# Two more row tile pairs of the down projection in a seven-product scheme, with the activation sums moved from GpSimd to VectorE and some transposes placed later

## The reference, cut to what matters

```python
h2 = rms_norm(x, ln_ffn_w[i])
u = causal_depthwise_conv(h2 @ w_up[i], conv_w[i], conv_b[i])
u_gate, u_val = jnp.split(u, 2, axis=-1)
x = x + (jax.nn.silu(u_gate) * u_val) @ w_down[i]
h3 = rms_norm(x, ln_ple_w[i])
x = x + jax.nn.sigmoid(h3 @ w_ple_gate[i]) * (p[i] @ w_ple[i])
```

## Time and profile before

| what | value |
|---|---|
| median of 3 runs | 1438.42 us (1438.13 to 1439.0) |
| profiled execution, its own time | 1438.39 us |
| its span | 1436.6 us, so 1.8 us lie around the span |
| mean granted TensorE clock | 0.999 of full speed |
| busy: TensorE matmul, VectorE, ScalarE, GpSimd | 1425.5, 985.1, 760.0, 216.9 us |

### The profile page before, as it was taken

How to read it: one execution, slowest core, us unless ns; L and a number is a source line. 1 busy time by engine, 2 the same in 40 slices (tenths; PEclk the granted TensorE clock), 3 DMA queues, 4 the chain that set the end, 5 groups by cost and what they waited for, 6 DMA issues and landing times.

```text
span 1436.6 us, 19705 instructions
## 1 busy us (share of the span) xinstructions
PE 1425.5 (99%) x7112; PEld 1212.1 (84%) x7112; DVE 985.1 (69%) x1180; ACT 760.0 (53%) x920; POOL 216.9 (15%) x153
## 2 busy tenths in 40 slices
PE   9999999999999999999999999999999999999997
PEld 7888888888888888888888888888888888888886
DVE  7576777845455455566777777777777887787755
ACT  7555655544444444555555555555555546554544
POOL 0044144100000000000101101111011531140000
PEclk9999999999999999999999999999999999999999
DMA  9765555456666655465666566565665656565653
GB/s 325 225 205 161 165 176 159 143 194 190 191 190 191 191 190 188 158 208 181 190 188 191 180 198 186 179 204 175 191 193 177 212 192 200 177 213 188 227 200 121
DMA packets 190875, 273.47 MB, mean 190 GB/s; under 512 B 11744, under 2 KB 103136, under 8 KB 190688
## 3 DMA queue, kind: packets, MB, share of 16 engines
q1 hardware_dynamic: 190384, 272.30, 59.6%
q10 hardware_dynamic: 432, 0.37, 0.1%
HBM read 270.53 MB, written 2.10 MB: 190 GB/s over the span
## 4 chain that ended last, share of the span: by engine, by line
PE 98%; DVE 1%; issue 1%; ACT 0%; ACTq 0%; POOLq 0%; POOL 0%; DVEq 0%
PE main L622 15%; PE main L624 15%; PE main L623 15%; PE aux L747 11%; PE main L747 11%; PE aux L756 6%; PE main L756 6%; PE main L672 3%; PE main L670 3%; PE main L671 3%; PE aux L670 3%; PE aux L672 3%; PE aux L671 3%; PE aux L788 1%; PE aux L818 1%
## 5 line engine op out<-in xcount | busy, mean ns | idle before, releaser
L1301 DVE TENSOR_TENSOR w_lo<-raw,w_hi 128x1024 fp32r<-128x1024 f32 (+1 forms) x490 | 612.4, 1260 | 394.5 <-ACT w_hi L1009 394.3
L1009 ACT ACTIVATE w_hi<-raw 128x1024 fp32r<-128x1024 f32 (+1 forms) x490 | 514.1, 1052 | 541.2 <-PE main L624 284.8
L622 PE MATMUL main<-w_hi,xT 128*128 128x512 f32 x702 | 276.8, 394 | 0.0
L624 PE MATMUL main<-w_hi,xT 128*128 128x512 f32 x702 | 273.6, 390 | 0.0
L623 PE MATMUL main<-w_lo,xT 128*128 128x512 f32 x702 | 273.6, 390 | 0.0
L747 PE MATMUL aux<-xT,w_hi 128*128 128x512 f32 x704 | 169.9, 391 | 0.0
L747 PE MATMUL main<-xT,w_hi 128*128 128x512 f32 x672 | 163.0, 391 | 0.0
L624 PEld LDWEIGHTS main<-w_hi,xT 128*128 128x128 f32 x702 | 131.9, 188 | 27.4
L622 PEld LDWEIGHTS main<-w_hi,xT 128*128 128x128 f32 x702 | 132.0, 188 | 27.0 <-issue 0.4
L623 PEld LDWEIGHTS main<-w_lo,xT 128*128 128x128 f32 x702 | 132.0, 188 | 26.1
L747 PEld LDWEIGHTS aux<-xT,w_hi 128*128 128x128 f32 x704 | 129.4, 188 | 25.2 <-issue 0.3
(11 more groups left out here) (270 smaller groups left out, 1770.7 us busy)
## 6 DMA issues: line engine op xcount, KB each, us to landing
raw<-in_w_up SPq DMA_DIRECT2D x336, 256.0 KB
raw<-in_w_in SPq DMA_DIRECT2D x136, 512.0 KB
raw<-in_w_down SPq DMA_DIRECT2D x84, 512.0 KB
raw<-in_w_out SPq DMA_DIRECT2D x32, 512.0 KB
raw<-in_w_ple_gate SPq DMA_DIRECT2D x32, 512.0 KB
raw<-in_w_branch_a SPq DMA_DIRECT2D x16, 512.0 KB
raw<-in_w_branch_b SPq DMA_DIRECT2D x16, 512.0 KB
raw<-in_w_in SPq DMA_DIRECT2D x15, 256.0 KB, 5.7
```

The source lines that it names most:

```text
L622: pe.matmul(acc, th, wh, start=first, stop=False)
L624: return pe.matmul(acc, tl, wh, start=False, stop=end)
L1009: ac.activation(w_hi[:, u % RING, :, 0:w], raw[:, u % RING, :, 0:w], ACT.Copy).then_inc(hi_full, 1)
L1301: dve.tensor_tensor(w_lo[:, u % RING, :, 0:w], raw[:, u % RING, :, 0:w], w_hi[:, u % RING, :, 0:w].bitcast(F32), ALU.subtract).then_inc(lo ...
```

## The change

- `SEVEN_AT` has six pairs a pass, at i = 5, 7, 10, 12, 15, 17, in place of five, at 5, 8, 11, 14, 17. So a seven-product pair is followed by one or by two plain pairs in turn, where there were two each time.
- Of the activation sums GpSimd keeps the join of high and low part (`join_act`). The four 128 by 128 additions go to VectorE (`act_sums`), in slot u - 4 (`SUMS_AT`; for the very first pair slot u - 2, as slot 8 of the stage is the earliest). ScalarE rounds them and VectorE takes the low part in slot u - 3. The results have two buffers, and the semaphore of the weight sums is split in two (`w_diffs`, `w_summed`).
- The transposes of the new x come one unit later, with the scaling behind them one slot later, and so do those of `obT` for head group 1, by two units.

```diff
-OBT = [PV[g] + 4 for g in range(2)]
+OBT = [PV[g] + 4 + 2 * g for g in range(2)]
...
-SEVEN_AT = ((5, 8, 11, 14, 17), (5, 8, 11, 14, 17))
+SEVEN_AT = ((5, 7, 10, 12, 15, 17), (5, 7, 10, 12, 15, 17))
 SEVENS = [down_unit(p, i) for p in range(2) for i in SEVEN_AT[p]]
 SEVEN = {u: q for q, u in enumerate(SEVENS)}
+SUMS_AT = {max(u - 4, DOWN + UK): q for q, u in enumerate(SEVENS)}
...
-X2_AT = {down_slot(n) + 1: n for n in range(NQ)}
+X2_AT = {down_slot(n) + 2: n for n in range(NQ)}
...
-        a_sums_hi = sb("a_sums_hi", [P, 4, P], F32R, ffn)
-        a_sums_lo = sb("a_sums_lo", [P, 4, P], F32R, ffn)
+        a_sums_hi = sb("a_sums_hi", [P, 2, 4, P], F32R, ffn)
+        a_sums_lo = sb("a_sums_lo", [P, 2, 4, P], F32R, ffn)
...
                 if part == 0:
                     ac.wait_ge(a_summed, q + 1)
-                    if q:
-                        ac.wait_ge(w_sums_done, 2 * q)
+                    if q > 1:
+                        ac.wait_ge(w_sums_done, 2 * (q - 1))
...
+                if s - 1 in SUMS_AT:
+                    sums_hi(SUMS_AT[s - 1], 0)
                 if s + 1 in SEVEN:
-                    sums_hi(SEVEN[s + 1], 0)
                     sums_hi(SEVEN[s + 1], 1)
...
-                        if s == at + 2:
+                        if s == at + 1 + norm:
                             hi_blocks(name, xT_hi, 4 * n, VCOL[vec] + 4 * n, xT_hi_ready)
...
+            def act_sums(q):
+
+                dve.wait_ge(a_joined, q + 1)
+                a = a_sums[:].rearrange("p k (b t) -> p k b t", t=P)
+                a11, a12, a21, a22 = a[:, 0, 0], a[:, 1, 0], a[:, 0, 1], a[:, 1, 1]
+                dve.tensor_tensor(a22, a21, a22, ALU.add).then_inc(a_sum_part, 1)
+                dve.wait_ge(a_sum_part, 3 * q + 1)
+                dve.tensor_tensor(a21, a11, a21, ALU.subtract).then_inc(a_sum_part, 1)
+                dve.wait_ge(a_sum_part, 3 * q + 2)
+                dve.tensor_tensor(a11, a22, a11, ALU.subtract).then_inc(a_sum_part, 1)
+                dve.wait_ge(a_sum_part, 3 * q + 3)
+                dve.tensor_tensor(a12, a12, a11, ALU.subtract).then_inc(a_summed, 1)
...
                     split_lo(s + LEAD)
+                if s in SUMS_AT:
+                    act_sums(SUMS_AT[s])
                 if s + 2 in SEVEN:
-                    weight_sums(s + 2)
-                if s + 1 in SEVEN:
-                    sums_lo(SEVEN[s + 1], 0)
+                    weight_diffs(s + 2)
+                if s - 1 in SUMS_AT:
+                    sums_lo(SUMS_AT[s - 1], 0)
                 for k in range(2):
                     if s - k in SEVEN:
                         sums_lo(SEVEN[s - k], k + 1)
...
-                        if s == at + 2:
+                        if s == at + 1 + norm:
                             lo_blocks(name, xT_lo, xT_hi, 4 * n, VCOL[vec] + 4 * n, xT_hi_ready, xT_ready, 4 * (NQ * norm + n))
...
-            def act_sums(u, q):
+            def join_act(u, q):
...
                 pool.tensor_tensor(a_sums[:], aT_hi[:, k:k + 2, :].bitcast(F32), aT_lo[:, k:k + 2, :].bitcast(F32),
-                                   ALU.add).then_inc(a_sum_part, 1)
-                pool.wait_ge(a_sum_part, done + 1)
-                pool.tensor_tensor(a22, a21, a22, ALU.add).then_inc(a_sum_part, 1)
+                                   ALU.add).then_inc(a_joined, 1)
```

More of the change, by code:

```diff
@@ L355, in build @@
             sem, ("pT_hi_ready", "pT_ready", "sig_ready", "emb_ready", "y_pre"))
[L357 to L360, removed]
+        w_diffs, w_summed, w_sums_hi_ready, w_sums_ready, w_sums_done = map(
+            sem, ("w_diffs", "w_summed", "w_sums_hi_ready", "w_sums_ready", "w_sums_done"))
+        a_joined, a_sum_part, a_summed, a_sums_hi_ready, a_sums_ready = map(
+            sem, ("a_joined", "a_sum_part", "a_summed", "a_sums_hi_ready", "a_sums_ready"))
         x2_turned, copied, combined = map(sem, ("x2_turned", "copied", "combined"))
@@ L454, in slot_split @@
                 if u - RING in SEVEN and it is None:
-                    sp.wait_ge(w_summed, 3 * (SEVEN[u - RING] + 1))
+                    sp.wait_ge(w_summed, 2 * (SEVEN[u - RING] + 1))
             def rows(u, w, k, col):
@@ L675, in act_block, with act_sum @@
                 return aT_hi[:, k, tb * P:(tb + 1) * P], aT_lo[:, k, tb * P:(tb + 1) * P]
-            def act_sum(k):
-                return a_sums_hi[:, k, :], a_sums_lo[:, k, :]
+            def act_sum(q, k):
+                return a_sums_hi[:, q % 2, k, :], a_sums_lo[:, q % 2, k, :]
             def ring_tile(u, t):
@@ L710, in down_seven @@
                     pe.wait_ge(a_sums_ready, q + 1)
-                    mm = triple(down_acc(2 * p + 1, 0), *act_sum(2), *ring_tile(u, 1), start=False, stop=False)
+                    mm = triple(down_acc(2 * p + 1, 0), *act_sum(q, 2), *ring_tile(u, 1), start=False, stop=False)
                 mm.then_inc(units_done, 1)
@@ L719, in down_sums @@
                 if half == 0:
-                    triple(product(p, 1), *act_sum(3), *sum_tile(0), start=first, stop=end)
-                    mm = triple(product(p, 3), *act_sum(1), *sum_tile(1), start=first, stop=end)
+                    triple(product(p, 1), *act_sum(q, 3), *sum_tile(0), start=first, stop=end)
+                    mm = triple(product(p, 3), *act_sum(q, 1), *sum_tile(1), start=first, stop=end)
                 else:
-                    triple(product(p, 2), *act_sum(0), *sum_tile(2), start=first, stop=end)
+                    triple(product(p, 2), *act_sum(q, 0), *sum_tile(2), start=first, stop=end)
                     mm = triple(down_acc(2 * p, 1), *act_block(2 * i + 1, 1), *sum_tile(3), start=False, stop=False)
@@ L1154, in sums_hi @@
                     ac.wait_ge(a_summed, q + 1)
-                    if q:
-                        ac.wait_ge(w_sums_done, 2 * q)
-                    ac.activation(a_sums_hi[:].rearrange("p k t -> p (k t)"), a_sums[:].rearrange("p k t -> p (k t)"),
+                    if q > 1:
+                        ac.wait_ge(w_sums_done, 2 * (q - 1))
+                    ac.activation(a_sums_hi[:, q % 2].rearrange("p k t -> p (k t)"), a_sums[:].rearrange("p k t -> p (k t)"),
                                   ACT.Copy).then_inc(a_sums_hi_ready, 1)
@@ L1160, in sums_hi @@
                     half = part - 1
-                    ac.wait_ge(w_summed, 3 * q + (1, 3)[half])
+                    ac.wait_ge(w_summed if half else w_diffs, 2 * (q + 1) if half else q + 1)
                     if q:
@@ L1553, in sums_lo @@
                     dve.wait_ge(a_sums_hi_ready, q + 1)
-                    dve.tensor_tensor(a_sums_lo[:].rearrange("p k t -> p (k t)"), a_sums[:].rearrange("p k t -> p (k t)"),
-                                      a_sums_hi[:].rearrange("p k t -> p (k t)").bitcast(F32), ALU.subtract).then_inc(a_sums_ready, 1)
+                    dve.tensor_tensor(a_sums_lo[:, q % 2].rearrange("p k t -> p (k t)"), a_sums[:].rearrange("p k t -> p (k t)"),
+                                      a_sums_hi[:, q % 2].rearrange("p k t -> p (k t)").bitcast(F32), ALU.subtract).then_inc(a_sums_ready, 1)
                 else:
```

21 lines of the change are left out of this document (7 added, 14 removed).

## The result

The changed kernel takes 1448.39 us (median of 6 runs, 1448.09 to 1449.34); the kernel before, run beside it, 1438.27 us. The ratio is 1.0070, 95% interval 1.0059 to 1.0081: 10.1 us slower. The prediction was 1445.4 us, its range ended at 1449.0.

What follows compares the result with a forecast made beforehand. TensorE's matmuls bound the kernel, so new waits are paid in full. From 1438.4 us, 12.1 of waits less 0.2 and 3.6 of gain gave 1446.7; less 1.3 for joins, 1445.4 us, range 1438.5 to 1449.

Steps and rivals of the forecast that it cites:

- the three waits: TensorE at the transposes of x (both passes) and `obT`: later places remove waits of 0.73, 0.73 and 0.78 us.
- (A): First half-sums of i = 10 and 15, behind the four additions: TensorE waits 0.73 us, 4 times; 0.15 at i = 5, pass 1.
- (D): The very first pair, with its own and i = 7's additions ahead of its half-sum: TensorE waits 1.66 us.
- one of its own signs of being wrong: The prediction called itself wrong if VectorE showed idle time in short cycles or half-sums waited under 0.1 us each.
- the step on the loads: Down projection: nothing queued on SyncE would add; loads wait for `w_summed` as before, their 2.1 us covered by VectorE's lateness.
- (B): Unit behind pairs i = 7, 12, 17: waits 0.82 us twice, 1.47 three times, the last 0.40.
- (C): Unit behind pairs i = 10 and 15: TensorE waits 0.24 us, four times.
- the joins: GpSimd's joins cost VectorE 1.07 us or nothing; early entry at most places but not all, so 1.3 us taken off.
- Rival 1: Joins hidden, GpSimd waiting until VectorE runs dry: about 5.0 us of waits, 1439.6 us; chance 0.23.
- Rival 2: VectorE's lead of three units (8 us) absorbs the debt, only the first pair waits a little: 1435.3 us; chance 0.10.
- Rival 3: ScalarE's waits for `a_summed` also hold back its copies, each short cycle costing 3 us: 1454 us; chance 0.07.

Runs made afterwards that it cites:

- run 7: The kernel before with only the transposes of x and of the head outputs moved as in the change: 1435.91 us, ratio to before 0.9982.
- Run 4: The changed kernel with weight sums reading the token buffer, and ring loads no longer waiting for these sums: 1441.99 us, -6.4 against the changed kernel.
- run 2: The changed kernel with five pairs a pass at the old places (5, 8, 11, 14, 17): 1436.71 us, -11.7 against the changed kernel.
- (3): The changed kernel with GpSimd's join cut to 2 x 8 columns for every pair but the first: 1437.84 us, -10.6 against the changed kernel.
- (9): The changed kernel with both the 8-column join and the loads that are not held: 1436.57 us, -11.8 against the changed kernel.
- run 10: The changed kernel with the four additions back on GpSimd behind its join, same lead of four units: 1451.34 us, +3.0 against the changed kernel.

## Why the prediction was right, and where it was not

**Sign and place.** Right: the three waits went (run 7 gives 2.5 us for them, the sum had 2.24), each short cycle runs VectorE into debt, and the new waits stand where (A) to (D) put them. The waits themselves sum to 11.7 us, against the 12.1 of the prediction. Its windows fit too: 12.5 us for a short cycle, VectorE busy for 93%. But one of its own signs of being wrong came: VectorE has idle time in the short cycles, 0.66 us in the one shown. That sign belongs to the step on the loads below.

**The terms.** By TensorE's start-to-start times: (A) 0.54, 0.52, 0.59 and 0.56 us for 0.73, and 0.19 for 0.15; (B) 0.75 twice for 0.82, 1.51, 1.58 and 1.68 for 1.47, and 0.36 for 0.40; (C) 0.22, 0.33, 0.27 and 0.31 for 0.24; (D) 0.47 + 1.11 for 1.66. Missing was what a wait does to the matmul behind it, here at the unit behind i = 12 (timeline of TensorE):

```profile
1165.79 0.39 PE L673 MATMUL main<-w_hi,a_sums_lo 128*128 128x512 f32 x1
1167.52 0.47 PE L671 MATMUL main<-w_hi,aT_hi 128*128 128x512 f32 x1 [1.34 <-DVE w_lo L1303]
1167.83 0.40 PE L672 MATMUL main<-w_lo,aT_hi 128*128 128x512 f32 x1
```

A matmul that was waited for shows 0.47 to 0.50 us in place of 0.39, and the second starts 0.08 to 0.11 us later than the pace; such a row stood in the earlier trace rows and I took only its start. At the seventeen waits this makes 1.7 us, against 0.1 us at the one first half-sum that waited before: 1.6 us more.

**Step that failed: the joins.** "I think it gets in early at most places but not at all; I take off 1.3 us." GpSimd got in at VectorE's first operation boundary at each of the ten joins that found VectorE at work, also at the half-size `w_lo` ahead of the weight sums, and no gap was needed. Rival 1 rested on the earlier trace rows, where a product let two subtractions pass; no join of the changed kernel did that. The sum without the deduction, 1446.7, plus 1.6 us for the second matmuls, is 1448.3 against 1448.4. That the agreement is so close is partly luck, by the next point.

**Step that failed: the loads.** "Nothing is queued on SyncE that would add" and, in (B), "the copy by ScalarE is waited for first (it starts when the unit before the half-sum ends)". The copy waits for its load, and the load for the last weight sum, which is itself late. Run 4 gives the split: without the hold (A) is 0.19, (B) 0.64 to 0.78 at five places and nothing at the last, (C) nothing. So 0.8 to 1.0 us of each (B) at i = 12 and 17, 0.35 of each (A) and all of (C) belong to the ring. My terms had nearly these sizes because I made VectorE start late there for another reason. Without the hold 6.4 of the 10 us are not there, and I had ruled it out in a sentence. The row for it was not a wait of before, where the loads cost 2.1 us, but the order of dependences: weight sum, 4.1 us to landing, 1.07 us of copy, against a period of 10.2 us.

**Rivals.** Rival 2, that the lead of three units absorbs the debt, fell with it: the lead is the ring, and the ring is held by the same engine. Rival 3 was too strong: ScalarE waited for `a_summed` 4.8 us in 4 waits, and the cycles lost 2.3 us and not 3.

**What the loss is.** Shown: it needs the short cycles (run 2), and in these the port (3) and the hold of the loads (4) each carry most of it, together little more (9), the hold mainly by passing on what the port makes late. Not shown: what each short cycle would cost with the ring one place deeper; that wasn't tried, since it changes the memory plan.

The Trainium skill (SBUF — State Buffer, section Who interferes with whom) states that a VectorE instruction with two SBUF inputs and a GpSimd instruction that reads SBUF block each other for whole instructions, and that the order of issue decides. The joins agree in kind: one of the two waits until the other's instruction is through. The price is a little under the whole join, 1.78 - 0.69 = 1.1 us where a join alone takes 1.30 us. An order of issue alone does not fit.

## What to carry to other kernels

When an engine is to get more work, write down the ring that its last result closes (release, load, copy, back to the engine) and compare its length with the shortest period, not with the mean one: a cycle of 12.5 us behind a period of 10.2 loses on every turn, and if the long cycle takes 16.07 against 15.64 nothing is given back. Put work that releases another engine behind the operation that frees the buffer; one line of schedule was worth 7 to 13 us here (the 13 with 3 us of the clock's in it) and no instruction more. Before an exchange between engines that share a port, price the exchange itself: most of the twelve joins cost VectorE more on the other engine (1.1 us each) than in its own queue (0.7 us). And measure the parts alone: the gain was in the three transposes, which the rest of the change had hidden.

## What the hardware showed that I had not expected

GpSimd was let in at VectorE's first operation boundary at the joins, even where VectorE had no gap at all, and the operation behind it took its own time plus 1.1 us. With five pairs the price was the same as with six. It is no strict rule: one join of run 10 let the running operation and the next one pass and took 2.81 us.

In run 10 the granted clock fell to 0.50 (1.2 GHz, the lower of the two levels) 1.2 and 1.4 us after TensorE had gone on from a wait of 2.74 and one of 2.79 us. It stayed there for a little over 3 us each time and cost 3.0 us in all, while a wait of 2.59 us elsewhere left it at 1.00. In the changed kernel, with waits of 1.7 us at most, it did not fall in this stage. A wait of this length can cost more than it lasts.
